# A hybrid layer with 32 experts on one core: stage borders rewoven, two expert matrices loaded one stage earlier, late tiles laid on multiples of 512 bytes

## The reference

```python
def hybrid_layer(x, past_k, past_v, past_logf, s0, conv_buf, p):
    h = rmsnorm(x, p["g_mix"])
    proj = jnp.einsum('btd,de->bte', h, p["w_in"])
    fq, fk, fv, flog, bq, bk, bv, bbeta, ba, bz, ga, gb = jnp.split(proj, offsets, axis=-1)
    ...
    y_a = fox_attend(fq, k_all, v_all, c_all[:, P:], c_all, pos_k[P:], pos_k)     # 8 heads of 64
    conv_out, new_buf = causal_conv(jnp.concatenate([bq, bk, bv], axis=-1), conv_buf, p["w_conv"])
    ...
    o_b, s_new = gdn_chunked(cq, ck, cv, g, beta, s0)                             # delta rule, 8 heads
    y_b = rmsnorm(o_b, p["g_onorm"]) * jax.nn.silu(bz)
    gate_a, gate_b = jnp.split(jax.nn.sigmoid(concatenate([ga, gb]) + p["b_gate"]), 2, axis=-1)
    branch_a = jnp.einsum('bte,ed->btd', y_a, p["w_br_a"])
    branch_b = jnp.einsum('bte,ed->btd', y_b, p["w_br_b"])
    x1 = x + jnp.einsum('btd,de->bte', gate_a * branch_a + gate_b * branch_b, p["w_out"])
    x2 = x1 + hier_moe(rmsnorm(x1, p["g_ffn"]), ...)                              # 32 experts, 2 per token

def run_block(args):                                                              # in hier_moe
    tok, e, wt = args
    xb = x_pad[tok]
    h = jax.nn.silu(xb @ w_e1[e]) * (xb @ w_e3[e])
    return (h @ w_e2[e]) * wt[:, None]
```

## Time and profile before

| | us |
|---|---|
| median of 3 runs | 1176.87 |
| lowest and highest | 1174.31, 1178.04 |
| the profiled execution, own time | 1176.7 |
| its span in the profile | 1175.0 |

### The profile page before, as it was taken

The page is one execution under the profiler, slowest core; times in us unless marked ns, Lnnn a source line. Parts: engine busy times, 40 slices in busy tenths (PEclk is TensorE's granted clock), DMA queues, the critical chain, the costliest instruction groups (busy, mean ns, idle before and its releaser), DMA issues. The chain is left out here.

```text
span 1175.0 us, 20594 instructions
## 1 busy us (share of the span) xinstructions
PE 1057.9 (90%) x8266; PEld 814.1 (69%) x8266; DVE 423.5 (36%) x988; ACT 367.8 (31%) x779; POOL 362.3 (31%) x408
## 2 busy tenths in 40 slices
PE   5999989899999989998999999998998877777787
PEld 4999988799998868888898755554554444444443
DVE  6687833972121743441232553212111001111215
ACT  5568733653323644552332531000000000000000
POOL 3433468622223343332453102212221111111100
PEclk9999989999999989999999989999999999999999
DMA  7423237165325411126230999999999999999998
GB/s 135 91 73 79 67 100 183 40 175 167 99 63 175 158 43 37 55 55 201 82 90 28 337 428 424 421 426 427 428 427 428 427 428 428 427 428 429 428 424 326
DMA packets 149709, 284.52 MB, mean 242 GB/s; under 512 B 43636, under 2 KB 118996, under 8 KB 132736
## 3 DMA queue, kind: packets, MB, share of 16 engines
q1 hardware_dynamic: 94288, 244.94, 53.5%
q10 hardware_dynamic: 49728, 27.59, 8.6%
q0 software_dynamic: 5616, 10.91, 2.4%
HBM read 266.81 MB, written 24.31 MB: 248 GB/s over the span
## 5 line engine op out<-in xcount | busy, mean ns | idle before, releaser
L2636 PE MATMUL bank<-e_w,b_xT 128*64 128x256 f32 x2048 | 233.0, 383 | 42.0 <-DMA e_w<-in_w_e 39.1
L499 PE MATMUL bank<-xhi,cv_w_hi 128*128 128x272 f32 x848 | 256.7, 303 | 11.5 <-ACT fox_cols L1349 3.5
L485 POOL TENSOR_TENSOR cv_w_lo<-cv_w_raw,cv_w_hi 128x1024 fp32r<-128x1024 f32 (+1 forms) x69 | 162.5, 2355 | 310.6 <-ACT cv_w_hi L478 310.3
L499 PE MATMUL bank<-xhi,cv_w_lo 128*128 128x272 f32 x848 | 246.8, 291 | 0.0
L499 PE MATMUL bank<-xlo,cv_w_hi 128*128 128x272 f32 x848 | 246.3, 290 | 0.0
L2636 PEld LDWEIGHTS bank<-e_w,b_xT 128*64 128x64 f32 x2048 | 149.8, 138 | 133.2 <-DMA e_w<-in_w_e 35.2
L499 PEld LDWEIGHTS bank<-xhi,cv_w_hi 128*128 128x128 f32 x848 | 162.0, 191 | 19.7 <-issue 13.2
L499 PEld LDWEIGHTS bank<-xlo,cv_w_hi 128*128 128x128 f32 x848 | 162.2, 191 | 1.2
L499 PEld LDWEIGHTS bank<-xhi,cv_w_lo 128*128 128x128 f32 x848 | 161.7, 191 | 0.0
L2681 DVE TENSOR_TENSOR b_hidden<-b_hidden,bank 128x256 f32<-128x256 f32 x32 | 13.5, 421 | 363.9 <-PE bank L2636 363.9
L2654 PE MATMUL bank<-e_w,b_hiddenT 128*64 128x512 f32 x512 | 116.9, 598 | 22.4 <-DVE b_hiddenT L2686 22.4
(11 more groups left out here) (457 smaller groups left out, 1610.7 us busy)
## 6 DMA issues: line engine op xcount, KB each, us to landing
e_w<-in_w_e SPq DMA_DIRECT2D x91, 2048.0 KB, 37.5
cv_w_raw<-in_w_in ACTq DMA_DIRECT2D x34, 512.0 KB, 4.2
e_w<-in_w_e SPq DMA_DIRECT2D x10, 1024.0 KB, 33.9
cv_w_raw<-in_w_in SPq DMA_DIRECT2D x18, 512.0 KB, 3.9
cv_w_raw<-in_w_br_b ACTq DMA_DIRECT2D x8, 512.0 KB, 4.2
o_raw<-in_w_out SPq DMA_DIRECT2D x16, 256.0 KB, 4.2
y_rows<-choice_rows SPq DMA_DIRECT2D x8, 512.0 KB, 6.9
g_values_gates<-g_z_stage ACTq DMA_DIRECT2D x12, 272.0 KB, 5.0
```

The source lines that it names most:

```text
L485: self.k.nc.gpsimd.tensor_tensor(self.wlo[:, s, 0:nk, :], self.raw[:, s, 0:nk, :], self.whi[:, c % OPS, 0:nk, :].bitcast(F32), ALU.subtract)\
L499: last = self.k.nc.tensor.matmul(self.bank(c, h)[:, 0:HALF], w, x[:, d, cols], start=(d == 0 and n == 0), stop=(d == nk - 1 and n == 2))
L2636: last = nc.tensor.matmul(k.bank[bank][sl[a], 0:FH], xT[:, d, :], w[u][:, d, FH * a:FH * a + FH], start=(d == 0), stop=(d == KD - 1))
```

## The change

- **Memory.** `sb_at` places a tile at an offset given by hand. All expert tiles, `x_rows`, `late` (mixing operands, output matrix) and the work tiles of the last stage now start at a multiple of 512 bytes. Small tiles of the early stages go to `small_ctx`, which is closed before the mixing stage.
- **Preload.** `w1` and `w3` of expert 0 have tiles of their own while the mixing stage runs, and SP issues their loads there, `w1` after the last but one piece of the output matrix, `w3` after chunk `GA0 + 12`. The last stage then starts with `w2` of expert 0 and the three of expert 1.
- **Loads of the mixing stage.** Eight pieces of `o_raw` and the rows `x_rows` at once become a sequence in which SP waits for `s_.half` of the mixing chunks; `x_prompt` is cut into four loads of 512 KB. `m_sum` is gone: the sum is made in `m_gate` and `part`, and DVE's wait for `low` is gone.
- **Convolution to delta.** ACT copies the first half of chunk `FOX0 + 1` in the stage before the barrier.
- **Middle of the delta stage.** POOL makes two `cv_w_lo` chunks and the queries 0 to 3 between steps of the recurrence. ACT makes `grow(2)` and `grow(3)` before `keep_values(0, 0)` and `grow(4)` behind `keep_values(0, 1)`.
- **Delta to head.** The first half of `GATE_B[0]` is copied at the end of the delta stage, with `gate_b` allocated earlier, and the scaling of `bgate` is done in the convolution's stage.
- **Head to fox.** The four spreads of the first pair of heads and their copies move into `head_rows` (bank 7, tile `f_bias`); `keep_keys` 2, 3 and 4 move from DVE to ACT; the low parts of heads 4 and 5 are made by POOL in `head_rows`, those of 6 and 7 by DVE at the start of `fox_heads`; the filler points are cut anew.

The diff, cut to its core:

```diff
+MATRIX = 4 * KD * 512
+PRE1_AT, PRE3_AT, LAST_AT = 40960, 177664, 212480
+ROWS_AT = PRE3_AT - 4 * 5 * D
+LATE_AT = ROWS_AT - 4 * (2 * KD * NT + 2 * KD * 512)
+FIRST_AT, WORK_AT = 6144, PRE1_AT + 2 * MATRIX
...
@@ convolution's stage, ACT
+                c_(nc.scalar.activation(k.bgate[:], k.bgate[:], ACT.Copy, scale=0.5))
...
+                a.wait_ge(s.half, 2 * FOX0 + 3)
+                nc.scalar.activation(k.fT[:, 1, 0:HALF], s.bank(FOX0 + 1, 0)[:, 0:HALF], ACT.Copy).then_inc(s.emptied_of(FOX0 + 1), 1)
+                s.ahead(a, FOX0 + 1, 0)
@@ delta_net
-    points = {..., "score4": 6, "keys": 4, "egs": 8,
+    points = {..., "score4": 8, "keys": 4, "egs": 6,
-                    for c, h in [(c0_ + 1, 0), (c0_ + 1, 1)] if name == "early" else fill.halves(name):
+                    for c, h in [(c0_ + 1, 1)] if name == "early" else fill.halves(name):
                 keep("grown")
+                grow(2)
+                grow(3)
...
+                keep_values(0, 0)
                 norms.square_on_scalar(s, 0)
                 norms.square_on_scalar(s, 1)
-                keep_values(0, 0)
...
                 keep_values(0, 1)
+                grow(4)
...
-                    if j == 1:
-                        for i in range(2, 5):
-                            grow(i)
...
+                keep_gate(k, s, GATE_B[0], 0, k.sgb[:, 0, :], 8)
+                s_.ahead(s, GATE_B[0], 0)
@@ delta_net, POOL
-                split_at = {26: "score0", 22: "score1", 17: "score2", 11: "score3"}
+                split_at = {22: "score1", 11: "score3", 8: "keys", 2: "grown"}
+                grow_at = {7: (0, 1), 5: (2,), 4: (3,)}
                 for j in range(31, 0, -1):
                     if j in split_at:
                         split(split_at[j])
+                    for i in grow_at.get(j, ()):
+                        grow_queries(i)
+                        qd.wait(g, GROW[i])
@@ head_rows
-    points.update({"x1": 8, "t1": 16, "t3": 8, "t4": 8})
+    points.update({"x1": 8, "t1": 8, "b1": 4, "b2": 4, "t3": 4, "t4": 12})
...
+            def spread(i):
+
+                if i >= 1:
+                    pe.wait_ge(biasc, i)
+                f = sides[i % 2]
+                nc.tensor.matmul(k.bank[7][:, 0:f.stop - f.start], k.selr[:, i // 2, :], k.ncs[:, f], start=True, stop=True)\
+                    .then_inc(bias, 1)
@@ head_rows, DVE
-            for t in (0, 1):
-                keep_keys(t)
-            for h in range(4):
+            for h in (0, 1):
                 gated(h)
-            for t in (2, 3):
-                keep_keys(t)
-            for h in (4, 5):
+                keep_keys(h)
+            for h in (2, 3):
                 gated(h)
-            low_part(0)
-            low_part(1)
-            keep_keys(4)
-            low_part(2)
-            low_part(3)
-            for h in (6, 7):
-                gated(h)
+            for h in range(LOW_HEADS):
+                low_part(h)
+                gated(LOW_HEADS + h)
@@ fox_heads
-            for h in range(LOW_HEADS, H - 1):
-                low_part(h)
             mask(0)
-            low_part(H - 1)
...
-            for i in range(4):
-                spread(0, i)
@@ mixed_rows, SP
-            for j in range(4):
+            o.load(sp, 0)
+            o.load(sp, 1)
+            sp.wait_ge(s_.half, 2 * (GA0 + 1))
+            o.load(sp, 2)
+            sp.wait_ge(s_.half, 2 * (GA0 + 2))
+            sp.dma_start(k.x[0:NS, 0, :], k.i["x_sample"][0]).then_inc(o.x_loaded, 16)
+            for j in range(3, KD):
+                sp.wait_ge(s_.half, 2 * (GA0 + 2 * j - 3))
                 o.load(sp, j)
-            sp.dma_start(k.x[0:NS, 0, :], k.i["x_sample"][0]).then_inc(o.x_loaded, 16)
-            sp.dma_start(k.x[:, 1:5, :], k.i["x_prompt"][0].rearrange("(t p) n -> p t n", p=128)).then_inc(o.x_loaded, 16)
-            for j in range(4, 2 * KD - 2):
-                o.load(sp, j)
+                if j < 7:
+                    sp.wait_ge(s_.half, 2 * (GA0 + 2 * j - 2))
+                    sp.dma_start(k.x[:, j - 2, :], k.i["x_prompt"][0, 128 * (j - 3):128 * (j - 2), :]).then_inc(o.x_loaded, 16)
+                o.load(sp, KD + j - 3)
+            load_weights(k, sp, "w_e1", k.w1, k.w1_loaded, 0, 0)
+            sp.wait_ge(s_.half, 2 * (GA0 + 13))
+            load_weights(k, sp, "w_e3", k.w3, k.w3_loaded, 0, 0)
+            o.load(sp, KD + 5)
@@ last stage, SP
-        for e in range(2):
-            load_up(k, sp, e, e)
-            load_down(k, sp, e, e)
+        load_down(k, sp, 0, 0)
+        load_up(k, sp, 1, 1)
+        load_down(k, sp, 1, 1)
```

190 lines of the change are left out of this document (115 added, 75 removed).

## The result

The changed kernel takes 1156.22 us (median of 4 executions, 1154.66 to 1159.95), against 1175.59 before: a ratio of 0.9839, 95% interval 0.9807 to 0.9872. That is 19.4 us less, where 27.5 were forecast; the time lies in the range. A second measurement of the same kernel, beside the experiments, gave 0.9821 (0.9801 to 0.9841) and 1156.04 us, against 1176.91 before.

The account below looks back on a forecast made before the run. The expert byte stream was taken to bound the end, so each microsecond won ahead of 652 us counts fully. Terms 4 + 2.5 + 9 + 2 + 6 + 6 = 29.5, less 2 for new waits, gave 27.5 off: 1149 us, range 1137 to 1164.

Parts of the forecast that it names:

- preload: Start of the last stage: two expert matrices loaded early put the stream 3.5 to 4.5 us ahead, taken as 4.
- alignment: Expert stream: tiles moved off starts at 192 modulo 512 save 2.5 us, bounds 0 and 5.5.
- convolution to delta: Start of the delta stage: PE's 2.3 us wait and 4.2 us half-clock loss go, together 6.5 us.
- middle of delta: Delta stage: waits and half clock of 5.4 us go, at a cost; with the border ahead of it 9 us.
- delta to head: Border into the head stage: 0.9 us of idle and some half clock go, 2 us, bounds 0.5 and 3.
- head to fox: Border before the fox heads: spreads, barrier idle, short waits and half clock save 6 us, bounds 2 and 7.
- mixing: Mixing stage: paced loads remove ACT's and PE's waits for late branch weights, 6 us, bounds 2 and 7.
- preload and alignment give nothing: Rival: the ring is full at the first release in both kernels and byte rate sets the pace; 1156, chance 0.12.
- The falls of the clock stay: Rival: PE's half-clock stretches stay at the borders of the front stages, 11 us less gain; 1160, chance 0.2.
- misses its borders: Rival: ACT is late in head and delta stages, PE waits at new places; 1161, chance 0.08.
- the full preload: Rival: early loading of two expert matrices gives its whole 9.8 us and tile placement its 5.5; 1140, chance 0.14.
- the starved mixing stage: Rival: paced loads delay branch weights in each of 8 column groups, 45 us lost; 1199, chance 0.04.

Follow-up runs that it names:

- x9: Changed kernel with low parts of heads 4 and 5 on VectorE, GpSimd's queries 2 to 4 behind the recurrence, ScalarE's grow(2) to grow(4) behind the logarithms: 1158.20 us.
- x1: Changed kernel with w1 and w3 of expert 0 loaded at the start of the last stage as before: 1158.23 us, ratio to before 0.9846.
- x4: Changed kernel with ACT's keep_values(0, 0) ahead of grow(2) and grow(3): 1155.81 us, ratio to before 0.9820.
- x11: Changed kernel with the head and fox stages as before, except that the gate's first copy stays in the delta stage: 1159.94 us, ratio to before 0.9865.
- x2: Changed kernel with all expert tiles, mixing operands, x_rows and work tiles 192 bytes further on: 1160.37 us, ratio to before 0.9871.
- x3: Changed kernel with the loads of the mixing stage in a burst as before, the two expert matrices still behind them: 1163.14 us, ratio to before 0.9905.
- x8: Changed kernel with the order of GpSimd and ScalarE in the middle of the delta stage as before, the early copy kept: 1160.11 us, ratio 0.9869.

## Why the prediction was right or wrong, point by point

| step | forecast us | measured us | from |
|---|---|---|---|
| preload | 4 | 0.5 and -0.6 | before with x9, x1 with x4, at equal clock |
| alignment | 2.5 | 1.6 | R to L |
| convolution to delta, middle of delta | 9 | 7.4 | S to P, 76.6 to 69.2 |
| delta to head | 2 | 1.4 | P to F, before to x11 |
| head to fox | 6 | 3.3 | P to F, x11 to changed |
| mixing | 6 | 5.7 to 6.0 | F to E 233.4 to 227.3, the fox stage's 0.1 to 0.4 taken off |
| toll of new waits | -2 | in the rows above | |
| sum | 27.5 | about 20 | medians 19.4 and 20.9 |

**What bounds the kernel: right.** The stream of bytes sets the end before and after, and what the front wins arrives in the total: S to E shortened by 17.5 and 18.4 us in the two traces, and the total by 19 to 21. The forecast was 7 us too low. The terms fell short by 9 to 10 us together, most of it in the preload (4), head to fox (2.7) and the first two borders (1.6), and the 2 us set aside for new waits covered a part.

**The preload: right in its mechanism, its term mis-sized.** The step that failed is "so the engines run dry there for 3 to 4 us": the prediction counted the one gap behind the first loads and let the rest of the saving reach the first release. But the issues at E + 38.8 and E + 39.5 also wait for PE, and the queue ran dry a second time ahead of them: one tile lands at E + 38.5, the next at E + 47.2, 8.7 us later where 4.9 us of bytes are needed. Measured are 3.2 to 3.5 MB unmoved there, of 4.2. (The step also has a slip in its sum: 677 in place of 688 is 11 us, not 9.8. In the traces all loads issued up to E + 10 have landed at E + 42.5 before and at E + 31.0 in the changed kernel.) The chance that went to "preload and alignment give nothing" (0.12) was nearer for the preload than the forecast itself. And two single profiles would have confirmed the wrong number: E to R 80.2 to 75.9 looks like 4.3 us, and is the clock of PE in the last stage. The sign that the prediction named, an interval from the first expert load to the end that shrinks by 10 or by 0 us, could not decide for the same reason: it shrank by 4.9 us in one trace and by 3.3 in the other.

**The alignment: right, the size inside its bounds.** 1.6 us against 2.5 (0 to 5.5), with the doubt of a single trace of before; x2 shows the effect itself beyond the spread. The pairs in rows 4 were a fair sample: 0.03 and 0.11 us for each matrix at 192, and x2 gives 4.9 us for some 82 of them, 0.06 each.

**Convolution to delta: the wait went, the gain didn't follow.** The idle of 2.3 us and the half clock at 155 are gone (0.66 to 1.00), as said. The step that failed is "Together 2.3 + 4.2 = 6.5": of it 2.3 arrive with GpSimd's order as before, 1.0 to 1.3 with the new one. It was treated as PE's own time, when PE had a wait for GpSimd 50 us later that takes up whatever PE wins ahead of it. The hand-followed figure (the product at 219 to 220.5) was too early by 1 to 2 us; which of its steps is short, no run shows.

**Middle of delta: the waits as said, the size in part by luck.** 5.1 to 5.4 us were measured, and the prediction's sum of what goes is 5.4. But that sum was meant before costs: with the 6.5 of the border it makes 11.9, of which the prediction kept 9 for the later `s_solved` and the new stall. Measured are 7.4 for both, with the loss at the border and not here. One of the three things named came back: the clock still falls (0.79 over 8 us), behind a stall at the kept values of 4.8 us, not 3 to 4. The prediction had expected this stall and yet named it as a sign that would prove its step wrong; in x4 this wait is gone from its place, another of 4.2 us stands in its stead, and the product comes no earlier.

**Delta to head: about right.** 1.4 against 2 (single traces, in a column that repeats within 1.1, and no run of its own), and the clock is at 1.00; the idle is 1.46 us, the barrier's own.

**Head to fox: the spreads are gone from behind the barrier as said, the barrier's idle and the clock's fall are not.** The step that failed is "with the keys moved to ACT and the order of DVE interleaved, about 1 goes ... a loss of 2.4 that goes if it no longer falls". The idle grew from 2.55 to 3.18 and the clock fell as before. In x11, with the head stage as before and the gate's first copy moved, the idle is 1.40, so the new order of the head stage costs 1.8 us of idle at this barrier. The prediction looked for lateness on ACT; it came on VectorE, through GpSimd. The trace of before had shown the cause: VectorE's low parts there took 3.56 us for two while GpSimd worked, against 1.34 a little later.

```profile
404.74 3.56 DVE L1698 TENSOR_TENSOR yb_lo<-conv_v,yb_hi 128x544 fp32r<-128x544 f32 x2
...
408.82 1.34 DVE L1698 TENSOR_TENSOR yb_lo<-conv_v,yb_hi 128x544 fp32r<-128x544 f32 x2
...
404.87 2.84 POOL L485 TENSOR_TENSOR cv_w_lo<-cv_w_raw,cv_w_hi 128x1024 fp32r<-128x1024 f32 x1 [2.98 <-ACT cv_w_hi L478]
```

**Mixing: right,** 6 us, of which 4.5 to 4.8 by the order of the loads (x3). The rest is open between the fall of the clock, which x3's trace lacks, and DVE's fewer waits, to which the prediction gave nothing.

**The rivals.** "The falls of the clock stay" came in part (two of four stay), "misses its borders" in part (convolution to delta, and head to fox), "the preload and the alignment give nothing" for the preload, and the full preload and the starved mixing stage not at all.

## What to carry to other kernels

A transfer taken out of a full queue is worth only the bytes that the queue doesn't then lose by running dry. So list the issue times and ask for each what it waits for, before the bytes are counted as time: where the later issues hang on another engine, little is won. A wait taken away shortly ahead of another wait mostly moves to that one (2.57 to 5.99 us in x8). A new order won 5 us while GpSimd had idle time to fill; once it was 90% busy over the stretch, three further orders moved the product by 1.5 us at most. Work that goes to an idle GpSimd has to be checked against VectorE's instructions of the same moment. Compare two profiles event by event, and ask first whether the clock was the same in both.
